# Dilated attention: four weight splits placed behind attention steps, and the first pool weight in two tiles with a rotation between

## What is computed

```python
u = rms_norm(h, mix_norm)
proj = u @ w_in                       # q, k, v (768 each), pz (512), gates (2048)
y_attn = dilated_mixture_attention(q, k, v) @ w_branch_attn
y_pool = multiscale_pool(pz, pool_w, pool_scale) @ w_branch_pool
merged = gates[:, :, 0] * y_attn + gates[:, :, 1] * y_pool
h = h + merged @ w_out
```

## Time and profile before

| what | value |
|---|---|
| three runs | 2288.86, 2289.5, 2292.99 us; median 2289.5 |
| the profiled execution | 2291.01 us, its span 2289.2 us |
| TensorE, matmuls busy | 2196.0 us, 96% of the span |
| VectorE, ScalarE, GpSimd busy | 1418.9 us (62%), 964.0 us (42%), 178.7 us (8%) |
| chain that ended last | TensorE 81%, VectorE 10%, ScalarE 4%, DMA 2% |
| mean granted clock of TensorE | 0.984 of full speed |

### The profile page before, as it was taken

How to read it: one execution, slowest core, us unless ns; L and a number is a source line. 1 busy time by engine, 2 the same in 40 slices (tenths; PEclk the granted TensorE clock), 3 DMA queues, 4 the chain that set the end, 5 groups by cost and what they waited for, 6 DMA issues and landing times.

```text
span 2289.2 us, 31979 instructions
## 1 busy us (share of the span) xinstructions
PE 2196.0 (96%) x13291; PEld 1940.5 (85%) x13291; DVE 1418.9 (62%) x2132; ACT 964.0 (42%) x1459; POOL 178.7 (8%) x155
## 2 busy tenths in 40 slices
PE   5988999999999899999989999999899999999998
PEld 3877888888898798898988999997778889899997
DVE  5676566556576667566446667654564545666674
ACT  3556343223256644463534444434443334443442
POOL 7210000000032100000010000002012001000000
PEclk8999999999999999999999999999999999999999
DMA  6442244555430212322312332333111332133230
GB/s 233 143 141 83 93 162 171 185 183 203 174 107 20 74 56 92 111 93 93 129 56 70 98 110 93 111 101 109 58 44 64 120 103 74 65 120 109 94 112 38
DMA packets 127734, 245.72 MB, mean 107 GB/s; under 512 B 4763, under 2 KB 36854, under 8 KB 127462
## 3 DMA queue, kind: packets, MB, share of 16 engines
q1 hardware_dynamic: 122832, 228.02, 29.5%
q0 software_dynamic: 4096, 15.28, 2.0%
q10 hardware_dynamic: 662, 0.37, 0.1%
HBM read 241.56 MB, written 2.10 MB: 106 GB/s over the span
## 4 chain that ended last, share of the span: by engine, by line
PE 81%; DVE 10%; ACT 4%; DMA 2%; issue 2%; POOL 0%; SPq 0%; DVEq 0%; ACTq 0%
PE PS L66 80%; DVE t L75 5%; ACT t L72 4%; DVE t L83 3%; DVE t L86 1%; DMA t<-in_ffn_w_dram 1%; PE PS L69 1%; DMA t<-in_w_ada_dram 1%; DVE t L79 1%; DMA t<-in_w_ff_dram 0%; DVE t L80 0%; DVE t L92 0%; POOL t L75 0%; DVE t L95 0%; DVE PS L75 0%
## 5 line engine op out<-in xcount | busy, mean ns | idle before, releaser
L66 PE MATMUL PS<-t,t 128*128 128x256 f32 (+4 forms) x12924 | 2145.4, 329 | 61.5 <-issue 14.2
L66 PEld LDWEIGHTS PS<-t,t 128*128 128x128 f32 (+2 forms) x12924 | 1896.5, 190 | 307.4 <-issue 72.7
L72 ACT ACTIVATE t<-t 128x512 f32<-128x512 f32 (+8 forms) x737 | 653.8, 904 | 947.4 <-DVE t L75 457.1
L75 DVE TENSOR_TENSOR t<-t,t 128x1024 fp32r<-128x1024 f32 (+9 forms) x692 | 777.9, 1141 | 387.8 <-ACT t L72 342.4
L72 ACT ACTIVATE t<-PS 128x512 f32<-128x512 f32 (+4 forms) x331 | 177.3, 550 | 245.2 <-PE PS L66 181.2
L75 POOL TENSOR_TENSOR t<-t,t 128x512 f32<-128x512 f32 (+2 forms) x71 | 87.5, 1233 | 1118.4 <-ACT t L72 949.6
L75 DVE TENSOR_TENSOR t<-t,PS 128x512 f32<-128x512 f32 (+2 forms) x134 | 83.2, 626 | 147.6 <-PE PS L66 141.4
L72 ACT ACTIVATE t<-t,t 128x256 fp32r<-128x256 f32 (+5 forms) x220 | 115.8, 536 | 92.2 <-DVE t L83 45.0
L83 DVE SCALAR_TENSOR_TENSOR t<-t,t,t 128x1024 f32<-128x1024 f32 (+2 forms) x157 | 145.2, 932 | 14.1 <-DMA t<-in_w_ada_dram 8.2
L83 DVE SCALAR_TENSOR_TENSOR t<-PS,t,t 128x512 f32<-128x512 f32 (+3 forms) x120 | 76.4, 642 | 99.2 <-PE PS L66 89.2
L69 PE MATMUL PS<-t,t 128*128 128x128 f32 (+1 forms) x367 | 59.7, 303 | 27.9 <-DVE t L79 6.7
(11 more groups left out here) (30 smaller groups left out, 154.3 us busy)
## 6 DMA issues: line engine op xcount, KB each, us to landing
t<-in_w_ff_dram SPq DMA_DIRECT2D x64, 1024.0 KB, 5.2
t<-in_ffn_w_dram SPq DMA_DIRECT2D x60, 1024.0 KB, 5.1
t<-in_w_ada_dram SPq DMA_DIRECT2D x36, 1024.0 KB, 5.8
t<-in_w_in_dram SPq DMA_DIRECT2D x13, 1024.0 KB, 5.2
t<-in_w_ada_dram POOLq DMA_DIRECT2D x24, 512.0 KB, 4.3
t<-in_swa_w_qkv_dram SPq DMA_DIRECT2D x6, 1024.0 KB, 5.6
t<-in_ffn_w_dram SPq DMA_DIRECT2D x8, 768.0 KB, 4.4
t<-in_w_in_dram SPq DMA_DIRECT2D x24, 256.0 KB, 3.7
```

Of the source, the lines that this page charges most:

```text
L66: return Instr(self.real and self.real.matmul(o, lhs, rhs, start=start, stop=stop, **more))
L72: return Instr(self.real and self.real.activation(o, src, func, **more))
L75: return Instr(self.real and self.real.tensor_tensor(o, a, b, op))
```

## The change

The first pool weight, 8 row blocks by 256 columns, becomes two weights of 4 row blocks (pz0a, pz0b), so its product runs over the first half of the rows for both tiles and then over the second half. The rotation of the last q tile stands behind "first weight, first tile", which is now a quarter of the product and was half of it. Four splits then get new places: k1a behind step 1, k1b behind step 3, pz1 behind step 6, ga0 behind step 8 (ahead of the output copies). In `act_qk(e, 1)` the last step now splits pz0b, and the step in front of step 13 still splits ga1.

```diff
@@ the plan @@
         qk_plan(1)
-        for n in range(2):
-            weight("pz", w_in[:, :, 2304 + 256 * n:2560 + 256 * n], 8, 256)
+        for u in range(2):
+            weight("pz", w_in[:, 4 * u:4 * u + 4, 2304:2560], 4, 256)
+        weight("pz", w_in[:, :, 2560:2816], 8, 256)
@@ act_qk (dve_qk alike, with dve_step) @@
             act_qk_parts(e, "dq", a, 1)
-            act_step(e, ws[3])
+            if a:
+                act_step(e, ws[3])
@@ new @@
+        def far_steps():
+
+            return {1: WX["qk"][3], 3: WX["v2"][0], 6: WX["pz"][0], 8: WX["pz"][1]}
@@ pe_dilated @@
-                    pe_linear(e, ("pz", 0), WX["pz"][0:1], [(0, 128), (128, 128)], h_of(n_mix),
+                    pe_linear(e, ("pz", 0), WX["pz"][0:2], [(0, 128), (128, 128)], h_of(n_mix),
                               lambda n, hf: (copied, ("pz", n)), mid={(F, 0, 0): lambda: pe_rotate(e, pending1, F, rot)})
                 if s == 13:
                     banks.only(0, 1, 2)
-                    pe_linear(e, ("pz", 1), WX["pz"][1:2], [(0, 128), (128, 128)], h_of(n_mix),
+                    pe_linear(e, ("pz", 1), WX["pz"][2:3], [(0, 128), (128, 128)], h_of(n_mix),
@@ act_dilated (dve_dilated alike, with dve_step and far[s] behind dve_d_soft) @@
             act_qk(e, 0)
-            act_step(e, WX["v2"][0])
             e.activation(WARM, EPSC, ACT.Exp).then_inc(misc_act, "warm")
...
+            far = far_steps()
             for s in range(16):
                 if s == 5:
                     ta.hand([(acc, ("dv", 3))])
                     act_qk(e, 1)
-                    act_step(e, WX["pz"][0])
                     act_qk_parts(e, "dq", 1, 2)
                     act_pz_copy(e, 0)
                 if s == 13:
-                    act_step(e, WX["pz"][1])
+                    act_step(e, WX["pz"][2])
                     act_pz_copy(e, 1)
                 act_d_turn(e, s)
                 if s < 13:
                     act_d_exp(e, s + 3)
+                if s in far:
+                    act_step(e, far[s])
                 if s == 8:
                     act_d_out(e, 0)
```

More of the change, by code:

```diff
@@ L2897, in dve_qk @@
             dve_qk_tile(e, "dq", a, 1)
-            dve_step(e, ws[3])
+            if a:
+                dve_step(e, ws[3])
         def d_banks(s):
@@ L3247, in dve_dilated @@
             dve_qk(e, 0)
-            dve_step(e, WX["v2"][0])
             dve_qk_tile(e, "dq", 0, 2)
@@ L3256, in dve_dilated @@
                     dve_qk(e, 1)
-                    dve_step(e, WX["pz"][0])
                     dve_qk_tile(e, "dq", 1, 2)
@@ L3261, in dve_dilated @@
                     e.memset(PZ[:, :, 0:16], 0.0).then_inc(misc, "edge")
-                    dve_step(e, WX["pz"][1])
+                    dve_step(e, WX["pz"][2])
                 if s < 13:
@@ L3267, in dve_dilated @@
                     dve_d_soft(e, s + 1)
+                if s in far:
+                    dve_step(e, far[s])
                 if s == 8:
```

## The result

| what | before | after |
|---|---|---|
| median | 2289.39 us (12 runs) | 2295.09 us (12 runs) |
| lowest to highest run | 2287.23 to 2292.99 | 2291.44 to 2295.86 |
| profiled execution, its span | 2291.01, 2289.2 | 2295.73, 2293.9 |
| from the first matmul of product v2 to the transposes of step 13 | 134.09 | 137.52 |
| from there to the end | 549.23 | 550.45 |

The ratio of after to before is 1.0022 with a 95% interval of 1.0013 to 1.0031: slower by about 5 us (3 to 7). Two profiled executions give the parts: +3.4 in the stretch that the change touches, +1.2 in the rest of the kernel, +0.1 ahead of both, together the +4.7 between the spans. The profiled execution of before took 1.6 us more than its median and that of after 0.6 more, which is why the spans differ by less than the medians (5.7).

The account below looks back on a forecast made before the run. In the attention stretch, TensorE, VectorE and ScalarE pass work in a ring, so a split costs by the step it lands in. Terms −0.2 + 0 − 2.1 − 1.3 + 2.3 + 3.7 + 1.3 = +3.7 gave 2293.2 us, range 2285.5 to 2297.5.

Parts of the forecast that it names:

- Part 1: Before scores 0: without k1a and k1b ahead of the last q tile, TensorE's whole 1.36 us wait is saved: −1.36.
- Part 5: First pz product to scores 8: fewer splits ahead of the q tile, less a 0.5 us wait for pz0b's lo: −2.1.
- 6, clock after scores 8: Behind scores 8: with the 3.44 us gap reduced, the clock stays up: −1.3 us, bounds 0 and −1.4.
- Part 2: k1a behind step 1: max 5 starts 1.15 us later, no slack, turn 3 moves by +1.15; bounds 0 and +1.8.
- Part 7: pz1 behind step 6: max 10 starts 3.4 us later, less 1.1 slack before scores 11: +2.3; bounds +1.2 and +3.4.
- 8, ga0: ga0 behind step 8: max 12, and scores 13 behind it, come later: +3.7 us; bounds +2.3 and +4.2.
- Part 9: Around scores 13: an idle gap of about 4.8 us drops TensorE's clock to half: +1.3 us, bounds 0 and +2.9.
- rival B: Slower by the clock: it falls in step 6 too (+1.3), step 8's fall lasts 6.8 us (+1.2): 2295.7; chance 0.2.
- 3, 4: k1b, loads: k1b behind step 3 is covered by some 50 us of products; weight loads come over 15 us early: 0 each.
- Rival A: The moved splits are hidden: parts 2, 7, 8 and 9 cost 0, leaving −4.8: 2284.7 us; chance 0.2.
- Rival C: Part 5's gain fails, TensorE waiting for pz0b's lo instead: up to 2.1 + 1.3 higher, at worst 2296.6; chance 0.05.

Follow-up runs that it names:

- filled: Kernel after with 14 idle matmuls of 512 columns in the gap before scores 13, splits unchanged: 2293.27 us, ratio 1.0015 against the kernel before.
- the filled versions: All four splits in idle places, plus 5, 4 and 8 idle matmuls in the first steps: 2283.54 us with two pool-weight tiles, 2283.92 with one.
- the version with every split in an idle place: Kernel after with k1a behind step 3, k1b behind step 4, pz1 behind the last q tile, ga0 in step 13: 2287.31 us, ratio 0.9992 against before.

## Why the prediction came out as it did

The forecast was 2293.2, +3.7 against before; measured were +5.7 between the medians and +3.43 in the stretch that the sum was made for. It held, because the terms that weigh most were read from the right rows. That the sum is within 0.3 of the stretch is in part luck: parts 1, 5 and 6 came out dearer than predicted and parts 2, 7, 8 and 9 cheaper. The median of 2295.09 lies just above the forecast's own range (to 2295.0) and near the 2295.7 of rival B, but not for B's reasons; the missing part lies behind the stretch (last point below). Term by term, in the stretch, with each version's times counted from the first matmul of product v2:

| part | predicted | measured | where it is seen |
|---|---|---|---|
| 1 and 2, k1a and k1b | −0.2 | +0.4 | turn 3 after 32.29 and 32.68; alone the whole stretch +0.5 |
| 3, 4: k1b, loads | 0 | 0 | no wait of TensorE |
| 5, the second removal | −2.1 | −1.9 | waits 0.57 and 0.73, before 3.44 |
| 6, clock after scores 8 | −1.3 | −1.0 | full clock |
| 7, pz1 | +2.3 | +1.8 | turn 7 to turn 9: 7.87 and 9.65; 1.61 before scores 11 |
| 8, ga0 | +3.7 | +3.4 | 4.43 before scores 13 |
| 9, clock in step 10 | +1.3 | +0.8 | turn 10 took 1.85; filled, −0.84 |

- **Part 1 is the step that failed.** "The whole 1.36 is saved and no more" was right up to turn 0, which comes 1.58 earlier. But the fall of the clock then also began earlier (1623.6 instead of 1627.6) and lasted 3.4 us longer. Scores 3 took 2.50 instead of 1.45, and at scores 4 only 0.53 of the gain is left. The term for the clock that part 9 has was missing here. That this fall cost about that much is shown by the filled versions, in which the same scores took 1.46. That it is longer because the wait is gone is borne out by the traces, not tested alone: it lasts 10.2 us in all nine traces that lack the wait and have no idle matmuls there, and 6.8 and 3.4 in the two that have it.
- **Part 2** was right in its mechanism: hi 1.47, lo 1.76, maximum 5 late, no slack. It cost 0.92 instead of 1.15 (0.53 ahead at scores 4, 0.39 behind at turn 3); with k1a behind step 3, in the version with every split in an idle place, turn 3 comes 0.99 sooner.
- **Part 5.** By the waits the gain was 2.1 as predicted; the product with its 0.3 more of weight loads and hand-over leaves 1.9. The new wait for pz0b's lo was 0.57, as taken (0.5). VectorE's piece of 3.66 us holds two halves of the q tile and a lo of 1024; at 0.70 each (the 1.40 for two, at 1682.41) and 1.22 that would be 2.62. It is 1.04 longer, next to GpSimd's multiply of 1.30. This agrees with the Trainium skill (SBUF — State Buffer, "Who interferes with whom"), which says that a VectorE instruction with two SBUF inputs and a GpSimd one that reads SBUF exclude each other. The 1.2 us that the prediction had worked out by it did not come, since TensorE reached that point later too, at 1689.6 instead of 1688.7.
- **Parts 7 and 8** were priced by hi plus lo in a row. That this is the mechanism, and VectorE's load the smaller part of it, is shown by the hi one step earlier (−3.8) and by the split taken out of step 8 (−4.4, the waits and the clock together). Part 7 was 0.5 too dear: maximum 10 started 2.95 us behind turn 7 where it was 0.19 before, so 2.8 later and not 3.4.
- **Part 9** was right in that the clock falls. The part of the fall on TensorE's own work was 1.6 us (at half clock), not 2.6.
- **Rival A** (hidden) fell: VectorE did idle in these steps (1.31 and 2.60 us), but while it waited for the hi, so the lo could not use it. **Rival B**'s additions did not come in step 6, and the fall in step 10 lasted 3.4 us. **Rival C** did not come.
- **What no part held** is the +1.2 in the rest of the kernel. The prediction put it at nothing because "behind the attention TensorE runs without a break"; it does so for 171 us, and the late fall lies at the first break. From turn 13 to the start of a group of 432 matmuls near the end (2131.60 before, 2136.78 after) it is 391.6 us in ten of the thirteen traces, to 0.1, and 393.3 in the three with the late fall: both of the kernel after, and that of the version with every split in an idle place. So the late fall costs 1.7 us. About 0.5 of it came back behind that, where the last fall started later in the kernel after (the two lines on the last transposes). The timeline of the kernel before at this place, against the last three lines of that of the kernel after:

```profile
1921.52 1.89 PE L66 MATMUL PS<-t,t 128*128 128x256 f32 x9 [0.81 <-DVE t L75]
1923.57 4.80 PE L66 MATMUL PS<-t,t 128*128 128x256 f32 x37 [0.15 <-POOL t L75]
1929.51 5.75 PE L66 MATMUL PS<-t,t 128*128 128x256 f32 x46 [1.15 <-DVE t L75]
```

The small idle pieces are alike, yet only the second kernel ran at half clock behind them (6.8 us from 1927.4), and the code there is the same. Why it fell there in two of the versions and not in the others stays open. The step 8 split is not what it takes: the version with all splits in idle places has none there. Since other falls differ between executions of one kernel, it is not shown either that this one belongs to the change. A forecast that goes by the stretch alone has to carry 1 to 2 us of uncertainty for it.

## What to carry to other kernels

- Work that is due much later is not free in a ring of engines because one of them is idle half the time. A split of two engines in a row costs hi and lo and what queues behind them (here 1.6 and 3.4 us of gap for two of them). Put it where all of these engines are idle together, before a long product or behind the last item of a batch, or put the first engine's half a step earlier.
- Where TensorE waits in short pieces, price the clock along with every wait, the ones removed too, and look at what comes behind. If the waits can't be avoided, idle matmuls in them are cheap: 17 of them were worth 3 us here. In unchanged code a longer or an additional fall made 0.7 and 1.7 us here, so a difference of that size between two traces needs the clock's rows beside it.
- Take the parts of a change one by one. The two tiles gained next to nothing, and the new places behind steps 1, 6 and 8 each cost time; what gained 3.6 to 3.8 us in the stretch was to take the splits from the old places, once they stood where all engines idle.

## What was not expected of the hardware

- The falls of TensorE's clock repeat only in part. Three of them are the same in two executions of the kernel after, to 0.1 us relative to the work; one near the start (6.8 and 10.2 us) and the last one are not. In the stretch they lasted 3.4, 6.8 or 10.2 us in every trace that has one. In the first steps it was 6.8 and 3.4 us in two versions with the same code there, for the same idle pieces of 1.05 to 2.12 us.
- Idle time taken away can cost clock. Without the 1.36 before scores 0 the next fall lasted 10.2 us in nine traces, against 6.8 and 3.4 with it. Without the 1.6 before scores 11 the next one lasted 6.8 instead of 3.4, but this is one trace, and with 0.20 there (the hi one step earlier) it lasted 3.4; so the second case is not shown.
- The Trainium skill (TensorE: Matmul & The Clock Gate, "Why this matters for your kernels") warns against idle gaps between bursts. The trace agrees for the gap of 4.43, and shows the same for single gaps no longer than 2.12 us (in the first steps) and of 0.80 (at 1925.03), behind which the clock stood at half for 10.2 and 6.8 us. Not every gap does it: the clock stayed full behind the 1.61 before scores 11, and in the kernel before behind the 0.81 at 1921.52.
